# Three edits in the mixers of a two-block model: paired scores with row-wise shifts, later weighting, and a state recurrence as one running sum

## What is computed

```python
# attention, 8 query heads over 2 key/value heads; keys are context and own tokens
s = einsum('bkgqd,bksd->bkgqs', q, k) * HEAD_DIM ** -0.5
p = softmax(s, axis=-1)
out = einsum('bkgqs,bksd->bkgqd', p, v)
# gated scan, once forward and once backward, chunk by chunk
s_new = exp(last[:, :, 0, :])[..., None] * s + einsum('bhsd,bhse->bhde', kc * exp(last - cum), vc)
o = einsum('bhtd,bhde->bhte', qc * exp(cum), s) + einsum('bhts,bhse->bhte', att, vc)
# and a Fourier mix of 4 groups
```

## Time and profile before

| what | us |
|---|---|
| median of 3 runs (2893.43 to 2899.86) | 2897.29 |
| the profiled execution's own time | 2901.79 |
| its span in the trace | 2899.9 |
| PE busy, share of the span | 2577.3, 89% |
| DVE, ACT, POOL busy | 891.4, 795.0, 837.4 |
| first branch stage (in the first block), in2_0, branch 0 | about 246 to 390, 911 to 1158, 1160 to 1383 |
| in2_1, branch 1 | 2050 to 2262, 2262 to 2450 |

### The profile page before, as it was taken

How to read it: one execution, slowest core, us unless ns; L and a number is a source line. 1 busy time by engine, 2 the same in 40 slices (tenths; PEclk the granted TensorE clock), 3 DMA queues, 4 the chain that set the end, 5 groups by cost and what they waited for, 6 DMA issues and landing times.

```text
span 2899.9 us, 38065 instructions
## 1 busy us (share of the span) xinstructions
PE 2577.3 (89%) x16618; PEld 1967.2 (68%) x16618; DVE 891.4 (31%) x1369; ACT 795.0 (27%) x1007; POOL 837.4 (29%) x310
## 2 busy tenths in 40 slices
PE   5998888999995999878889999999699777899998
PEld 3875556777773777335768888888467434678786
DVE  3003246244245232653341101111442454411113
ACT  3122233122123311332331112122322443322222
POOL 2231232333331111541222232222112342343342
PEclk8898899999997999887999999999799888999999
DMA  6441023344442100100111112111110101222221
GB/s 178 141 152 45 24 88 143 147 148 171 154 166 75 44 22 1 43 2 33 71 56 61 59 59 73 59 51 57 55 44 8 43 2 60 75 99 89 101 86 60
DMA packets 42954, 220.53 MB, mean 76 GB/s; under 512 B 4073, under 2 KB 12921, under 8 KB 19493
## 3 DMA queue, kind: packets, MB, share of 16 engines
q1 hardware_dynamic: 35624, 200.52, 18.9%
q10 hardware_dynamic: 7164, 17.57, 2.4%
HBM read 212.05 MB, written 6.03 MB: 75 GB/s over the span
## 4 chain that ended last, share of the span: by engine, by line
PE 71%; DVE 9%; ACT 4%; issue 1%; DMA 1%; POOL 1%; ACTq 0%; DVEq 0%; POOLq 0%
PE PS L651 56%; PE PS L654 2%; PE PS L1810 2%; DVE s_states L1417 1%; PE PS L1035 1%; DVE tmp L584 1%; DVE a_lo L576 1%; PE PS L1059 1%; PE PS L712 1%; PE PS L1616 1%; PE PS L1723 1%; DVE hid_lo L865 1%; PE PS L1041 1%; PE PS L536 1%; ACT w_hi L748 1%
## 5 line engine op out<-in xcount | busy, mean ns | idle before, releaser
L1901 POOL TENSOR_TENSOR w_lo<-raw,w_hi 128x2048 fp32r<-128x2048 f32 (+2 forms) x146 | 650.0, 4452 | 1678.2 <-ACT w_hi L748 1678.2
L651 PE MATMUL PS<-a_hi,w_hi 128*128 128x512 f32 (+1 forms) x2104 | 697.6, 376 | 135.1 <-DVE a_lo L576 53.8
L651 PE MATMUL PS<-a_lo,w_hi 128*128 128x512 f32 (+1 forms) x2104 | 678.1, 367 | 0.0
L651 PE MATMUL PS<-a_hi,w_lo 128*128 128x512 f32 (+1 forms) x2104 | 674.8, 365 | 0.0
L651 PEld LDWEIGHTS PS<-a_hi,w_hi 128*128 128x128 f32 x2104 | 361.1, 191 | 234.0 <-issue 136.9
L651 PEld LDWEIGHTS PS<-a_hi,w_lo 128*128 128x128 f32 x2104 | 362.0, 191 | 65.8
L651 PEld LDWEIGHTS PS<-a_lo,w_hi 128*128 128x128 f32 x2104 | 362.0, 192 | 61.5 <-issue 0.5
L748 ACT ACTIVATE w_hi<-raw 128x2048 fp32r<-128x2048 f32 (+2 forms) x146 | 270.4, 1852 | 393.2 <-PE PS L651 200.1
L651 PE MATMUL PS<-hid_hi,w_hi 128*128 128x512 f32 (+1 forms) x784 | 266.2, 376 | 31.9 <-DVE hid_lo L865 31.2
L651 PE MATMUL PS<-hid_lo,w_hi 128*128 128x512 f32 (+1 forms) x784 | 264.2, 374 | 0.0
L651 PE MATMUL PS<-hid_hi,w_lo 128*128 128x512 f32 (+1 forms) x784 | 263.7, 373 | 0.0
(11 more groups left out here) (196 smaller groups left out, 2605.7 us busy)
## 6 DMA issues: line engine op xcount, KB each, us to landing
raw<-in_w_ada SPq DMA_DIRECT2D x48, 1024.0 KB, 6.9
raw<-in_w_ff SPq DMA_DIRECT2D x32, 1024.0 KB, 4.8
raw<-in_w_in SPq DMA_DIRECT2D x27, 1024.0 KB, 4.8
raw<-in_w_gate SPq DMA_DIRECT2D x22, 1024.0 KB, 4.7
raw<-in_w_up SPq DMA_DIRECT2D x22, 1024.0 KB, 4.8
raw<-in_w_down SPq DMA_DIRECT2D x16, 1024.0 KB, 4.7
raw<-in_w_out SPq DMA_DIRECT2D x12, 1024.0 KB, 5.0
raw<-in_w_down SPq DMA_DIRECT2D x8, 768.0 KB, 4.3
```

What stands on the lines that cost most here:

```text
L651: mm = p.matmul(ps[:, dst], wv[:, k, idx * P:(idx + 1) * P], av[:, k, dst], start=first, stop=last)
L1901: pool.tensor_tensor(w_lo[:, m % 2, 0:kt, 0:ncol], src, w_hi[:, m % 2, 0:kt, 0:ncol].bitcast(F32), ALU.subtract).then_inc(s_lo.sem, 1)
```

## The change

It has these parts.

- **Scores.** One unit is now both heads of a group (one query tile, one key part): two products into the two banks of PS[3], every second tick, and one DVE maximum over both (128x2x384). PE waits for the maximum of the unit before. 40 units in layer 0, 32 in layer 1.
- **Shifts.** After the last unit PE turns the negated maxima into rows (two products per group, 16 and 8 in all) with head h of group g at partitions 64*(g%2)+32*h, one row per query tile. After the stage, DVE multiplies these rows by a selector (`shift_dve`: one instruction of 2048 values per partition in layer 0, 1024 in layer 1) into `shift`; L1041 becomes a product over 4 rows (2 for context groups). POOL's block-diagonals of the second block go.
- **Tables.** The four DMAs move into `norm_act`, ahead of the row tiles (`early_loads`), and PE's wait for them to the first use of `turn`.
- **Values.** Values and sums of the second block's groups alternate between two banks; inverse and weighting come two steps later; the last step's exponentials are not added on POOL but summed by PE in two more products.
- **States.** The decay columns are spread by ACT to one value per state element (`spread`), ACT copies the updates from PSUM to `states` laid out as [element][chunk], and one `tensor_tensor_scan` on DVE makes all states (1536 values per partition, 1024 in the first block). The states are then read by PE with a step of 24 (16) values. The first chunk's product with a zero state goes. SCAN_TICKS 14 becomes 12; attention's stream gets two more positions.

```diff
-        small, _ = put("small", [P, 128])
+        small, _ = put("small", [P, 160])
-        bdiag2 = [over("bdiag2_0", [P, 2, SEQ], hi_at + 8 * K, F32R), over("bdiag2_1", [P, 2, SEQ], hi_at + 12 * K, F32R)]
+        shift = over("shift", [P, 4, SEQ], hi_at + 8 * K, F32R)
-            take("decay", T // CH, 2)
+            room["spread"] = over(f"{tag}_spread", [P, T // CH * HD], qb_at)
             act_split(a, rank[where[then][0]] + 1)
+            if then in ("in2_0", "in2_1"):
+                early_loads(a, int(then[-1]))
...
+        def values_ps(plan, g):
+            half = 0 if plan["causal"] else g % 2
+            return PS[1][:, 512 * half:512 * half + 512]
+        def sums_ps(plan, g):
+            half = 1 if plan["causal"] else (g + 1) % 2
+            return PS[1][:, 512 * half:512 * half + 512]
+        def att_ticks(plan):
+            return len(plan["steps"]) + 4
...
-                    mm = p.matmul(ps[:, lo:n], ones_r[:], bd[g % 2][:, h, lo:n], start=False, stop=not causal)
+                        r0 = 64 * (g % 2) + 32 * h
+                        mm = p.matmul(ps[:, lo:n], ones_r[r0:r0 + grp["nq"], :], shift[r0:r0 + grp["nq"], g // 2, lo:n],
+                                      start=False, stop=True)
...
-                    p.wait_ge(S("weighted").sem, S("weighted").at(g))
+                if first and g > 0 and not causal:
+                    p.wait_ge(S("taken").sem, S("taken").at(g))
...
+                for part in range(1 if causal else 2):
+                    for h in range(2):
+                        src = acc(plan, g, h) if part == 0 else pt[:, s % 2, h, :]
+                        mm = p.matmul(sums_ps(plan, g)[grp["heads"][h]["rows"], 0:n], ones[:, 0:HD], src[:, 0:n],
+                                      start=part == 0, stop=causal or part == 1)
...
-        SCAN_TICKS = 14
+        SCAN_TICKS = 12
...
-                        nc.vector.scalar_tensor_tensor(states[:, b_, :], states[:, a_, :], s.room[f"decay{n % 2}"][:, a_:a_ + 1],
-                                                       bank(a_ % 4)[:, a_ // 4 * HD:a_ // 4 * HD + HD], ALU.mult, ALU.add).then_inc(tell.sem, 1)
+                if k == 9:
+                    v.wait_ge(S("copied").sem, S("copied").at(n + 1))
+                    nc.vector.tensor_tensor_scan(states, s.room["spread"][:], states, 0.0, ALU.mult, ALU.add).then_inc(S("states").sem, 1)
...
+                    nc.scalar.activation(spread[:, :, 0:1], wide(total[:, 0:1]), ACT.Copy, scale=0.0).then_inc(a_step.sem, 1)
+                    for lo, src in pieces:
+                        nc.scalar.activation(spread[:, :, lo:lo + src.shape[-1]], src, ACT.Exp, scale=c).then_inc(a_step.sem, 1)
+                if k == 9:
+                    a.wait_ge(S("updates").sem, S("updates").at(n + 1))
+                    for j in range(4):
+                        nc.scalar.activation(states.rearrange("p e (t j) -> p j t e", j=4)[:, j], blocks(bank(j)[:, 0:HD * s.nt], HD),
+                                             ACT.Copy).then_inc(tell.sem, 1)
...
-                if k == 12:
+                if k == 10:
                     p.wait_ge(S("states").sem, S("states").at(n + 1))
...
-                        return p.matmul(bank(j)[HD * (r % 2):HD * (r % 2) + HD, o:o + CH], states[s.rows(r), 4 * t + j, :],
+                        return p.matmul(bank(j)[HD * (r % 2):HD * (r % 2) + HD, o:o + CH], states[s.rows(r), :, entry - 1],
...
-            return SCORES_AT + len(att2[l]["units"])
+            return SCORES_AT + 2 * len(att2[l]["units"]) + 3
...
-            p.wait_ge(S("tables").sem, S("tables").at(64))
+                        if j == 0:
+                            p.wait_ge(S("tables").sem, S("tables").at(64))
...
-                    if u >= 2:
-                        p.wait_ge(S("max").sem, S("max").at(u - 1))
+                    if u >= 1:
+                        p.wait_ge(S("max").sem, S("max").at(u))
+                    for h, hd in enumerate(grp["heads"]):
+                        mm = p.matmul(PS[3][:, 512 * h:512 * h + n], hd["q_r"][:, c:c + P], hd["k_r"][:, k0:k0 + n],
+                                      start=True, stop=True)
+                    mm.then_inc(S("scores").sem, 1)
+                if tick == early_ticks(l) - 1:
+                    p.wait_ge(S("negated").sem, S("negated").at(len(plan["groups"])))
+                    for g in range(len(plan["groups"])):
+                        for h in range(2):
+                            r0, o = 64 * (g % 2) + 32 * h, 64 + 8 * g + 4 * h
+                            mm = p.matmul(PS[3][r0:r0 + 32, P * (g // 2):P * (g // 2) + P], small[:, o:o + 32], ident[:],
+                                          start=True, stop=True)
```

More of the change, by code:

```diff
@@ L913, in attention_plan @@
             for g in by_tile:
-                for h in range(2):
+                for h in range(2 if which == "first" else 1):
                     for i in range(groups[g]["nq"]):
@@ L930, in attention_plan @@
                     units_at[2 * f + 1 + k] = []
[L931 to L933 removed]
+                if g + 1 < len(groups) and causal:
                     u0, m = end_unit[g], end_unit[g + 1] - end_unit[g]
@@ L985, in acc, with adds_to @@
             return acc1[:, h, :] if plan["causal"] else acc2[:, g % 2, h, :]
+        def adds_to(plan, s):
+            g, j, first, last = plan["steps"][s]
+            return 2 * (s - g) if plan["causal"] else 2 * (s - 2 * g - int(last))
+        def att_ticks(plan):
+            return len(plan["steps"]) + 4
         def att_pos(plan, end, k):
-            return end * (k + 1) / (len(plan["steps"]) + 3)
+            return end * (k + 1) / (att_ticks(plan) + 1)
         def att_pe(p, st, plan, end=1.0):
@@ L1076, in att_pe @@
             yield att_pos(plan, end, 0)
-            for s in range(len(steps) + 2):
+            for s in range(att_ticks(plan)):
                 if s > len(steps):
@@ L1224, in att_act @@
             yield att_pos(plan, end, 0)
-            for s in range(len(steps) + 2):
+            for s in range(att_ticks(plan)):
+                if not causal and s >= 2 and s - 2 < len(steps) and steps[s - 2][3]:
+                    inverses(steps[s - 2][0])
                 if s < len(steps):
@@ L1236, in att_act @@
                             strip(hd["strip"])
-                if 1 <= s <= len(steps) and steps[s - 1][3] and (not causal or s == len(steps)):
+                if causal and s == len(steps):
                     inverses(steps[s - 1][0])
@@ L1285, in rows, with place, lane @@
                 return slice(self.dk * r, self.dk * r + self.dk)
+            def place(self, t):
+                return self.tiles.index(t)
+            def lane(self, j):
+                return 3 - j if self.back else j
             def att(self):
@@ L1880, in early_dve, with shift_dve @@
                         v.wait_ge(S("rotated").sem, S("rotated").at(j + 1))
-                if tick >= SCORES_AT:
-                    maximum(tick - SCORES_AT)
+                u, odd = divmod(tick - SCORES_AT, 2)
+                if 0 <= u < len(plan["units"]) and not odd:
+                    maximum(u)
                 yield
+        def shift_dve(v, l):
+            S = lambda n: local(("early", l), n)
+            made_ = local(("att", 1 + l), "shift")
+            n = len(att2[l]["groups"]) // 2
+            v.wait_ge(S("rows").sem, S("rows").at(1))
+            o = COLS["sel"][0]
+            own_tile = cols[:, o:o + 4].unsqueeze(1).unsqueeze(3).to_broadcast([P, n, 4, P])
+            rows = PS[3][:, 0:P * n].rearrange("p (g q) -> p g q", q=P).unsqueeze(2).to_broadcast([P, n, 4, P])
+            nc.vector.tensor_tensor(shift[:, 0:n, :].rearrange("p g (i q) -> p g i q", q=P), rows, own_tile,
+                                    ALU.mult).then_inc(made_.sem, 1)
         qn_scaled = small[:, 44:46]
```

164 lines of the change are left out of this document (86 added, 78 removed).

## The result

The changed kernel takes 2849.57 us (median, 2845.57 to 2853.86) against 2897.22 us beside it: ratio 0.9837, 95% interval 0.9815 to 0.9858. That is 47.6 us faster; 94 were forecast, and the forecast range ended at 2842. The profiled execution has a span of 2851.3 us against 2899.9, 48.6 us less, so its trace can be read for where they went. Ratios are to runs of the kernel before taken beside each kernel's own, and 0.0010 is 2.9 us.

A forecast was written before the change was run, and what follows sets the result against it. PE work bounds the scores, a chain round the engines the branches; tables 29.8, scores 38.5, minus 2 for row transposes, plus 28 for branches and GLA, give 94.3 us gained: 2803 us, range 2772 to 2842.

The forecast's parts named there:

- Tables: Start of in2_0 and in2_1: earlier table loads remove PE's idle wait; 29.8 us gained, between 24 and 32.
- Scores: Inside in2_0 and in2_1: 72 paired scores save 0.54 us each, eight smaller 0.5; 38.5 us, lower end 8.6.
- Branches: Second block's two branch stages: fewer DVE links and less PE work, less copies and shift; 27 us, range 0 to 60.
- Rival 4: Branches' state layout: strided states read and written at half speed, loads 38 us and copies 14; 2855 us, chance 0.12.
- the 4 us for `shift_dve`: Head of DVE's chain in the branches: the new shift instruction takes at most 3.0 and 1.5 us; 4 us charged.
- 3.8 us of DVE per half: Scan halves in the branches: 7.3 us of links replaced by a 3.5 us sum; 30 us over eight halves.
- Rival 1: Branches give nothing, DVE's and POOL's saved work replaced by ACT's copies and PE's extra sums; 2831 us, chance 0.2.
- 2: Rival 2: the branches give all, 60 us instead of 28; 2771 us, chance 0.12.
- 5: Rival 5: strided state loads and writes at several times their time make the kernel slower, e.g. 2931 us; chance 0.04.
- rival 3: Scores in in2_0 and in2_1: the paired products run one after the other; 2833 us, chance 0.07.
- outputs stand two ticks earlier: Scan outputs in the branches: coming two ticks earlier gives no more than the 27 us branch sum and 1 for GLA.
- signs: Trace checks: copies over 0.9 us suggest rival 4; a longer branch or in2_0 losing under 25 us means wrong.

The follow-up runs named there:

- e9: The changed kernel with the old link chain, one-bank attention bookkeeping and POOL's block-diagonals put back, leaving tables and score pairs: 0.9783 of the kernel before.
- e3: The changed kernel with states in rows of 64 for both ACT's copies and PE's loads (result wrong): 0.9713 of the kernel before.
- e6: The changed kernel with only PE's loads of the states in rows, copies keeping their step (result wrong): 0.9793 of the kernel before.
- e7: The changed kernel with the loops of ACT's copies exchanged, innermost step 4 values instead of 24, same layout and result: 0.9793 of the kernel before.
- e11: The changed kernel with two copies per half instead of four, each writing two neighbouring values together, same result: 0.9778 of the kernel before.
- e14: The changed kernel with the shift product over 32 rows instead of 4 or 2, the added rows zero: 0.9796 of the kernel before.
- e10: The changed kernel with POOL's block-diagonals back instead of the shift rows, all else kept: 0.9782 of the kernel before.
- e16: The changed kernel with block-diagonals back and states in rows for copies and loads (result wrong): 0.9694 of the kernel before, 2809.74 us.
- e17: The changed kernel with two-lane copies and block-diagonals, plus the one-bank attention bookkeeping of before: 0.9816 of the kernel before.
- e4: The changed kernel with PE's outputs at tick 12 and DVE's reading at 13 again (14 ticks): 0.9900 of the kernel before.
- e13: The changed kernel with a useless product added before each attention product of the second block, same result: 1.0328 of the kernel before.
- e15: The changed kernel with both two-lane copies and block-diagonals back, result kept: 0.9718 of the kernel before, 2815.91 us.

## Why the prediction was wrong

**Tables: right.** 17.3 + 12.5 forecast, 17.8 + 14.1 measured.

**Scores: right.** With 1 us for the row transposes taken off in each layer, 20.5 and 16 were forecast; of the 37.6 and 31.4 us won ahead of the branches, 19.8 and 17.3 are not the tables'. The period of a pair is 2.68 us, as forecast (2.1 + 0.58). e9, with tables and pairs alone, gained 63 us against 68 by these two terms.

**Branches: wrong, 27 us forecast, 19.8 lost.** Two steps failed, the first in two ways.

1. *"four copies of 384 values, each under the 0.59 us of a 512-value pass, 0.5 us, so 2.0 per half."* The 0.5 was read from ACT passes without a step, and the step of 24 values was left to a rival with 0.12. A copy took 0.97 us on the chain. And the sum charged them only twice: *"they show where nothing covers them, in the last half of each layer (2 x 2.0)"*. They stood on the chain in all eight halves: 30.5 us where 4 were charged. Even at 0.5 us a copy that overlap would have failed, for in e3 the copies stand on the chain in all eight too, 1.5 to 1.6 us each time. PE's loads of the states with a step were put at nothing: 6.3 us by their records, 13 by e6. The argument against it, DVE's copy of 24 values with a step of 32 in 0.18 us, was no evidence: 24 values are too few for a price per value to show above the instruction's own time. Rival 4 forecast 2855 and came within 6 us of the result, but with its parts the wrong way round: it charged the loads 38 us and the copies 14; removing them gave 13 and 21. The rule it drew on called four fp32 values a free stride, which e7 does not bear out; two neighbours written together cost no more than rows, as e11 shows. It deserved the larger chance.

2. *"with 4 rows each, in different row groups, the two may overlap: 0.3 us off each of 56 steps, 17 us of PE."* The pair does overlap, and saves 0.24 us at 2.4 GHz. What failed is that I took this as a gain for PE ("counts in part where PE is the last: 5"). Counted at a fixed clock it is one; but PE is granted less clock with the thin product. e14 puts that alone at 12 us; e9 and e10, which also drop `shift_dve`, give 11 and 16. No rival had this.

With both out of the way (e16) the branches take 221.1 and 175.7 us, 24.9 less than before, against the 27 forecast, and the whole is 2810 against 2803. That the two sums agree is in part luck: e16 has neither the 4 us for `shift_dve` nor the 5 for the thin product in it, its copies stand on the chain in every half, and no run measures the rest (3.8 us of DVE per half, the extra sums, the spread) term by term; e17 shows that they hang together.

**Rival 1** (2831), **2** and **5** did not come; **rival 3** is refuted by the score records. That outputs stand two ticks earlier was called worth nothing of its own; e4 gives it 18 us.

Two readings in the prediction were off without consequence: the stages that it says make up 650 of 2900 us add up to 870, and PE's lower share in the branches is 76%, not 77%. Its signs worked: a copy over 0.9 us spoke for rival 4, and a branch that got longer for its being wrong, while in2_0 lost 37.6 us, more than the 25 asked.

## What to carry to other kernels

A cheaper instruction on PE need not be a gain: in a stretch where PE waits for other engines, a product with 4 rows instead of 32 cost 12 us here. So compare the granted clock of the whole window before and after, and try the product with more rows. When a layout is turned so that one engine can run along it, price the step for every other engine that writes or reads it, from an instruction with hundreds of values, and look whether two neighbours can be written together. Before you call work covered, ask what the next engine in the chain waits for: here the copies were on the chain in every half. And test parts in pairs: here one edit was worth nothing or 28 us depending on another.

## What was not expected of the hardware

- The granted clock differed with the number of rows of a product whose time is the same: 0.43 us per pair with 4 and with 32 rows, yet 0.76/0.75 against 0.78/0.80 of the clock, and 12 us. It did not go by PE's busy share: e13 had the largest and the lowest clock, 0.70/0.67. How the chip comes to it no run here shows.
- ACT writing fp32: 0.41 us for 384 values in rows, 0.73 with a step of 4, 0.99 with a step of 24; 0.80 for 768 values in pairs of neighbours, with a step of 512 in PSUM that costs next to nothing (768 adjacent values: 0.81).
- 92 records of PE's outputs with weights at a step of 24 values: 6.04 us against 5.12, at 1.2 GHz.
- DVE's running sum over 1536 values took 3.36 us in all eight halves of the change. In e3 and e15 it took 3.92 to 3.97 us in three halves of eight, each time with an addition of POOL still under way when it began; in the other five it took 3.36. And an addition of POOL that began during the sum took 4.09 us (3.89 in the change) where 1.27 is usual, though the profile's times of POOL are rough. In e3 (timeline from 1160 to 1165, branch 0):

```profile
1159.10 2.62 POOL L1190 TENSOR_TENSOR acc<-acc,pt 128x512 f32<-128x512 f32 x2 [0.73 <-ACT pt L1234]
1161.01 3.92 DVE L1445 TENSOR_TENSOR_SCAN s_states<-s_spread,s_states 128x1536 f32<-128x1536 f32 x1 [7.83 <-ACT s_states L1560]
1161.91 4.09 POOL L1190 TENSOR_TENSOR acc<-acc,pt 128x512 f32<-128x512 f32 x1 [0.19 <-ACT pt L1234]
```

In these rows the long sum and POOL's additions lengthen each other, and PE's sums wait for the additions: a price that the prediction of one sum for 23 links did not have. What it costs in all no run here separates.
